# Inverse roots of all norms on ScalarE, shifts added by ScalarE, a seventh row buffer and a halved queue scratch

## The chip, the cores and the metric

The kernel runs on one core of a Trainium2 chip. The metric is device time in microseconds, the median of several runs; lower is better.

## The reference, cut to what matters

Two transformer blocks work on 512 positions of width 1024, all in float32. The change touches every norm and the gather of the experts:

```python
def rms_norm(x, g):
    y = xf * lax.rsqrt(jnp.mean(xf * xf, axis=-1, keepdims=True) + EPS)
    return y * g

# block one
h = rms_norm(x, norm1_g)
q, k = rms_norm(q, q_norm_g), rms_norm(k, k_norm_g)      # per head of 64
h2 = rms_norm(x, norm2_g)                                # ahead of w_up, w_down
# block two: the same norm with a gain and a shift that come from c
h  = rms_norm(x, g_norm1) * (1 + scale1) + shift1
q, k = rms_norm(q, g_q_sb), rms_norm(k, g_k_sb)
y_sb, y_ml = rms_norm(y_sb, g_out_sb), rms_norm(y_ml, g_out_ml) * sigmoid(o)
h2 = rms_norm(x, g_norm2) * (1 + scale2) + shift2
x  = x + gate2 * peer(h2, ...)
# peer: each position picks 128 of 16384 experts (8 heads, 16 each)
u, vv = expert_u[idx], expert_v[idx]                     # rows of 1024 numbers each
y = sum_k gate_k * gelu(h2 . u_k) * vv_k
```

## The kernel before

**The two halves.** The positions are worked in two halves of 256 (`half(0)`, `half(1)`). Within a half the activations lie transposed, as eight tiles of 128 features by 256 positions. Each half runs the same blocks of weights in the order of the list `SEQ`: query, key and value of block one (`Q1`, `K1`, `V1`), convolution inputs, attention with three weight products filled in between its heads, the projections, `UP` and `DN` (16 weight blocks each), then block two: `Q2`, `K2`, `QKM`, the two mixers with `V2`, `VM`, `OM` filled in, `WO2`, and the queries `PQ` of the expert choice. SyncE loads each weight block (1 MiB) into a ring of four as soon as the block four places back has been used. In half 0 there are 24 further blocks (`ADA`), which VectorE sums up for the modulation.

**A norm.** ScalarE squares the eight tiles, TensorE sums them over the partitions with a matrix of ones (bank 4), ScalarE takes `Sqrt` of the mean (`rms_root`, line 1096, or the end of `rms_squares`, line 1115), VectorE inverts it with `reciprocal` (`rms_inverse`, line 1638) and makes the eight tiles of `H`: `rms_scale` (line 1642) with one product each, `rms_modulate` (line 1648) with a product (line 1652) and, of the same engine, the addition of the shift (line 1655). TensorE's next weight block begins on tile 0 as soon as it is there and takes the tiles in order. There are eight such norms, numbered `a_` 0 to 7: 0 and 4 ahead of `Q1`, 1 and 5 ahead of `UP`, 2 and 6 ahead of `Q2`, 3 and 7 ahead of `PQ`. Those numbered 2, 3, 6 and 7 are modulated. In half 0 TensorE has other work beside norms 1 and 2: narrow products for the modulation (line 908).

**A head norm.** `head_squares` squares the tiles as they are evacuated, TensorE sums per head, `head_root` (line 1144) takes `Sqrt` of all heads at once, `head_inverse` (line 1658) inverts on VectorE, TensorE spreads the result over the partitions (`head_spreads`, line 642) and VectorE scales (line 1664). It is called for the queries during `K1`, for the keys during `V1`, and for block two during `QKM`. The two output norms of block two (lines 1401 and 1405 on ScalarE, 2011 and 2022 on VectorE) are small: 16 and 8 columns.

**The experts.** Each position needs 128 rows of u and v. For the four tiles of 128 positions these are 4 times 128 indirect DMAs of 1 MiB, called rows 0 to 511 below, issued by GpSimd (POOL) in that order; each brings one u and one v for 128 positions. VectorE takes the dot product with u (line 1537), ScalarE applies Gelu (line 1053), VectorE multiplies by the gate (line 1549), and adds v times that number (line 1566), or TensorE does so for every second row from row 198 on (line 563), for which ScalarE makes a diagonal matrix (line 1046). In half 1 the experts of the first half's positions run as steps of two rows, one after most weight blocks (`tick`; 99 steps). Their rows go round through six buffers of 8 KiB per partition (`uv0`). Rows 204 to 511 go round through 16 buffers: the six, the four weight blocks' places and six places of the activations. This table of buffers is written out ahead of time:

```python
NUV0, NUV1, WIDE = 6, 16, 204
CHANGE = ENTRIES.index(WIDE)
for _p, _e in enumerate(ENTRIES):
    _r = _p % NUV0 if _p < CHANGE else (_p - CHANGE + NUV0) % NUV1
```

GpSimd waits at `CHANGE` until TensorE has used the last weight block and the last scores are copied, and before each issue until the row that held the buffer has been consumed. It also stores the finished tiles of the output (line 517), 13 entries after their own; the buffer they are stored from is the one that the entry 16 places on takes.

## Time and profile before

| | us |
|---|---|
| median of three runs | 2686.62 (2684.66 to 2686.92) |
| the profiled execution, its device time | 2682.38 |
| its span, first to last instruction | 2680.7 |
| mean granted clock of TensorE | 0.901 |
| TensorE busy | 2168.2 (81%) |
| VectorE busy | 1762.0 (66%) |
| ScalarE busy | 640.1 (24%) |
| GpSimd busy | 785.5 (29%) |

Each engine's busy time is given against the span. The shares are averages over stages of different kind, so the stretches have to be read apart: the windows view gives busy times of each engine, TensorE's granted clock (1.00 is 2.4 GHz, 0.50 is 1.2 GHz) and the share of time in which the DMA engines moved data. In the timeline a number in brackets is the time that the engine stood idle before the instruction, with the instruction that ended it. One product of 128 by 128 by 256 in float32 shows as two MATMUL records of 0.215 us spacing at full clock.

### The profile page before, as it was taken

What the parts mean: (1) busy time and instruction counts of PE and PEld (TensorE: products, weight loads), DVE (VectorE), ACT (ScalarE), POOL (GpSimd) and SP (SyncE); (2) the same over time, 40 slices, a digit from 0 to 9 for tenths busy, and PEclk for the clock granted to TensorE, in tenths of its full rate; (3) what the DMA queues carried; (4) which work ended last, traced back from release to release, by engine and by line L of the source; (5) the groups of instructions that cost most, each with busy time, mean ns of one, the idle gap of its engine ahead of it and who ended that gap; (6) DMA issues with size and microseconds to landing.
All of it is one profiled execution on the core that took longest, in us unless ns stands there. A gap on an engine that the chain in (4) does not pass through costs nothing. (4 is left out here: it accounts for less than half of the span.)

```text
span 2680.7 us, 26294 instructions
## 1 busy us (share of the span) xinstructions
PE 2168.2 (81%) x9024; PEld 1627.7 (61%) x9024; DVE 1762.0 (66%) x3674; ACT 640.1 (24%) x1495; POOL 785.5 (29%) x541
## 2 busy tenths in 40 slices
PE   8999999999999999898999997988554554545544
PEld 6787788887788778677888776877111221212211
DVE  4662110002428769687777686676999999999987
ACT  2103302102332310563231134533111111111110
POOL 0000000000000234244433332224754555545552
PEclk9999999999999999899999998989877777778776
DMA  6774334443245699798999975468999999999997
GB/s 253 286 268 142 123 117 148 156 157 110 95 144 220 250 366 411 257 338 326 400 421 421 380 277 199 188 233 331 419 421 406 422 422 421 422 389 421 421 422 311
DMA packets 114868, 798.33 MB, mean 298 GB/s; under 512 B 13328, under 2 KB 16528, under 8 KB 19248
## 3 DMA queue, kind: packets, MB, share of 16 engines
q0 software_dynamic: 74736, 540.57, 49.6%
q1 hardware_dynamic: 40000, 256.09, 25.9%
q8 instruction: 72, 1.18, 0.2%
q14 instruction: 60, 0.49, 0.1%
HBM read 790.27 MB, written 6.34 MB: 297 GB/s over the span
## 5 line engine op out<-in xcount | busy, mean ns | idle before, releaser
L588 PE MATMUL PS<-reg,ring 128*128 128x256 f32 x6016 | 1360.9, 385 | 39.6 <-DVE reg L1655 10.8
L588 PEld LDWEIGHTS PS<-reg,ring 128*128 128x128 f32 x6016 | 1147.0, 193 | 222.5 <-issue 44.3
L536 POOL DMA_INDIRECT uv<-in_expert_uv,experts x318 | 520.9, 1638 | 1551.9 <-DVE experts L1519 842.7
L1566 DVE SCALAR_TENSOR_TENSOR acc<-uv,coef,acc 128x1024 f32<-128x1024 f32 x256 | 328.9, 1285 | 9.4 <-DVE coef L1549 0.3
L563 PE MATMUL PS<-reg,spare 128*128 128x512 f32 x224 | 156.6, 853 | 199.9 <-ACT spare L1046 199.9
L1537 DVE CUSTOM_DVE_ANT_0 uv<-uv,h_tok 128x1024 f32<-128x1024 f32 x222 | 263.7, 1220 | 36.5 <-DMA uv<-in_expert_uv,experts 36.2
L563 PEld LDWEIGHTS PS<-reg,spare 128*128 128x128 f32 x224 | 58.1, 275 | 297.4 <-issue 297.4
L563 PE MATMUL PS<-uv,spare 128*128 128x512 f32 x240 | 149.3, 768 | 95.8 <-ACT spare L1046 95.8
L1053 ACT ACTIVATE acts<-dots 128x2 f32<-128x2 f32 (+2 forms) x194 | 39.5, 204 | 762.0 <-DVE dots L1537 710.3
L536 POOL DMA_INDIRECT reg<-in_expert_uv,experts x114 | 159.3, 1398 | 206.2 <-PE PS L563 151.9
L563 PE MATMUL PS<-ring,spare 128*128 128x512 f32 x152 | 109.6, 874 | 85.0 <-ACT spare L1046 85.0
L563 PEld LDWEIGHTS PS<-uv,spare 128*128 128x128 f32 x240 | 54.7, 241 | 188.8 <-issue 188.8
L1841 DVE TENSOR_TENSOR reg<-PS,reg 128x256 f32<-128x256 f32 x16 | 6.5, 422 | 224.4 <-PE PS L588 224.4
L1537 DVE CUSTOM_DVE_ANT_0 reg<-reg 128x1024 f32<-128x1024 f32 x96 | 115.1, 1223 | 29.0 <-DMA reg<-in_expert_uv,experts 29.0
L563 PEld LDWEIGHTS PS<-ring,spare 128*128 128x128 f32 x152 | 40.0, 278 | 151.8 <-issue 151.8
L585 PE MATMUL PS<-ring,reg 128*128 128x256 f32 x512 | 121.1, 393 | 0.0
L536 POOL DMA_INDIRECT ring<-in_expert_uv,experts x80 | 96.6, 1207 | 75.0 <-PE PS L563 57.0
L1537 DVE CUSTOM_DVE_ANT_0 uv<-uv,reg 128x1024 f32<-128x1024 f32 x96 | 112.5, 1221 | 3.1 <-DMA uv<-in_expert_uv,experts 3.1
L585 PEld LDWEIGHTS PS<-ring,reg 128*128 128x128 f32 x512 | 98.9, 197 | 17.5 <-issue 3.9
L1053 ACT ACT_TABLE_LOAD x60 | 77.0, 1283 | 85.7 <-issue 57.2
L1735 DVE SCALAR_TENSOR_TENSOR uv<-ring,silu_c,uv 128x256 f32<-128x256 f32 x168 | 81.5, 485 | 6.0
L1549 DVE TENSOR_TENSOR coef<-acts,gates 128x2 f32<-128x2 f32 (+2 forms) x194 | 30.4, 157 | 82.5 <-ACT acts L1053 78.7
(264 smaller groups left out, 2133.1 us busy)
## 6 DMA issues: line engine op xcount, KB each, us to landing
ring<-in_weights SPq DMA_DIRECT2D x228, 1024.0 KB
uv<-in_expert_uv,experts POOLq DMA_INDIRECT x318
kv_half<-reg SPq DMA_DIRECT2D x1, 2052.0 KB, 11.2
reg<-kv_half SPq DMA_DIRECT2D x1, 2052.0 KB, 14.3
reg<-in_x_t SPq DMA_DIRECT2D x2, 1024.0 KB, 5.4
reg<-in_sub_t SPq DMA_DIRECT2D x2, 1024.0 KB, 4.9
toep<-rel_neg SPq DMA_DIRECT2D x16, 128.0 KB
x_tokens<-reg SPq DMA_DIRECT2D x2, 1024.0 KB, 10.0
```

The lines of the kernel that those rows point to most:

```text
L536: gp.indirect_dma_start(UV[r], None, a["expert_uv_2"], bass.IndirectOffsetOnAxis(ap=experts[:, e % 256:e % 256 + 1], axis=0))\
L563: mm = pe.matmul(PS[:, 6 + j, :], diag[:, n % 4, :], UV[BUF[s]][:, D + 512 * j:D + 512 * j + 512], start=begins, stop=ends, **LAX)
L585: mm = pe.matmul(out_tile(n, t), mv[:, t * P:(t + 1) * P], w, start=first and k == 0, stop=last and k == KT - 1)
L588: mm = pe.matmul(out_tile(n, t), w[:, t * P:(t + 1) * P], mv, start=first and k == 0, stop=last and k == KT - 1)
L1053: act.activation(acts[:, s0 % 16:s0 % 16 + s1 - s0], dots[:, s0 % 16:s0 % 16 + s1 - s0], ACT.Gelu)\
L1537: dve.tensor_tensor_reduce(out=u, in0=u, in1=H2[s // 256][:, s // NSLOT % 2, :], scale=1.0, scalar=0.0, op0=ALU.mult, op1=ALU.add, accum_o ...
L1549: dve.tensor_tensor(coef[:, q:q + w], acts[:, q:q + w], gates[:, s0 % 256:s0 % 256 + w], ALU.mult)\
L1566: dve.scalar_tensor_tensor(acc[:, :], v, c, acc[:, :], ALU.mult, ALU.add).then_inc(acc_done, 1)
L1735: dve.scalar_tensor_tensor(ac, ring[:, n % NRING, k, :], silu_c[:, k:k + 1], ac, ALU.mult, ALU.add)\
L1841: dve.tensor_tensor(x[:, k, :], out_tile(n, t), x[:, k, :], ALU.add).then_inc(evac_sem(n, t), 1)
```

## The change

The inverse root becomes two activations on ScalarE, `Ln` and then `Exp` with a factor of -0.5, for the eight norms, the six head norms and the two output norms in each half; VectorE's 18 reciprocals go. The shift of the modulated norms is added by ScalarE (`rms_shift`). All early loads of the `Sqrt` set become early loads of the set with `Exp` and `Ln`. In `head_spreads` TensorE now also waits for the scaling of the heads before at the first spread. The queue scratch, memory in which GpSimd's DMA queue keeps its descriptors, is declared at 8192 bytes per partition (16384 where nothing is declared), and the freed 8 KiB hold a seventh row buffer: 7 buffers up to row 203, 17 from row 204 on.

```diff
-NUV0, NUV1, WIDE = 6, 16, 204
+NUV0, NUV1, WIDE = 7, 17, 204
...
                 if j == 0:
                     pe.wait_ge(rr_done, 3 * hf + which + 1)
-                else:
+                if hf or which or j:
                     pe.wait_ge(hn_done, NQK * hf + 8 * which + 2 * j)
...
             def rms_root(a_):
                 act.wait_ge(rms_mm, KT * (a_ + 1))
-                act.wait_ge(h_done, KT * a_)
-                act.activation(rstd[:, :], PS[:, rms_bank(a_), 0:T], ACT.Sqrt, bias=epsc[:, :]).then_inc(rms_sqrt, 1)
+                if a_:
+                    act.wait_ge(h_done, KT * a_)
+                act.activation(rstd[:, :], PS[:, rms_bank(a_), 0:T], ACT.Ln, bias=epsc[:, :]).then_inc(rms_ln, 1)
+                act.wait_ge(rms_ln, a_ + 1)
+                act.activation(rstd[:, :], rstd[:, :], ACT.Exp, scale=-0.5).then_inc(rms_rec, 1)
+
+            def rms_shift(a_, g):
+                n0 = KT * (2 * (a_ // 4) + g)
+                for k in range(KT):
+                    act.wait_ge(h_pre, n0 + k + 1)
+                    act.activation(H[:, k, :], H[:, k, :], ACT.Identity, bias=mod[:, 24 * g + k:24 * g + k + 1]).then_inc(h_done, 1)
...
             def rms_squares(a_, src, ready):
-                ready_for(ACT.Sqrt)
+                ready_for_soft()
...
                 if at:
                     act.wait_ge(hb_done, at)
-                act.activation(hroot[:, :], PS[:, 5, 0:T], ACT.Sqrt, bias=epsc[:, :]).then_inc(rt_done, 1)
+                act.activation(hroot[:, :], PS[:, 5, 0:T], ACT.Ln, bias=epsc[:, :]).then_inc(rt_done, 1)
+                act.wait_ge(rt_done, 3 * hf + which + 1)
+                act.activation(hroot[:, :], hroot[:, :], ACT.Exp, scale=-0.5).then_inc(rr_done, 1)
...
                     rms_squares(2, X[0], lambda k: evac_wait(act, NO[0, DN, 4 * (k // 2) + 3], k % 2))
+                rms_shift(4 * hf + 2, 0)
...
-                act.activation(mean_sb[:, :], mean_sb[:, :], ACT.Sqrt, bias=epsc[:, :], scale=1.0 / HD2).then_inc(mix_root, 1)
+                act.activation(mean_sb[:, :], mean_sb[:, :], ACT.Ln, bias=epsc[:, :], scale=1.0 / HD2).then_inc(mix_root, 1)
+                act.wait_ge(mix_root, 2 * hf + 1)
+                act.activation(mean_sb[:, :], mean_sb[:, :], ACT.Exp, scale=-0.5).then_inc(mix_rec, 1)
...
                 if hf == 0:
-                    ready_for(ACT.Sqrt)
+                    ready_for_soft()
                     rms_root(4)
...
-            def rms_inverse(a_):
-                dve.wait_ge(rms_sqrt, a_ + 1)
-                dve.reciprocal(rstd[:, :], rstd[:, :]).then_inc(rms_rec, 1)
...
             def rms_modulate(a_, g, src):
-                n0 = KT * (2 * (a_ // 4) + g)
                 dve.wait_ge(rms_rec, a_ + 1)
                 for k in range(KT):
                     dve.scalar_tensor_tensor(H[:, k, :], src[:, k, :], gs[:, g, k:k + 1], rstd[:, :],
                                              ALU.mult, ALU.mult).then_inc(h_pre, 1)
-                    dve.wait_ge(h_pre, n0 + k + 1)
-                    dve.tensor_scalar(H[:, k, :], H[:, k, :], mod[:, 24 * g + k:24 * g + k + 1], None, ALU.add)\
-                        .then_inc(h_done, 1)
-
-            def head_inverse(hf, which):
-                dve.wait_ge(rt_done, 3 * hf + which + 1)
-                dve.reciprocal(hroot[:, :], hroot[:, :]).then_inc(rr_done, 1)
...
-    nc = bacc.Bacc("TRN2", target_bir_lowering=False, num_devices=1)
+    nc = bacc.Bacc("TRN2", target_bir_lowering=False, num_devices=1, dynamic_dma_scratch_size=8192)
```

## Rows read from the trace of the kernel before

**Rows 1.** The page: busy time of each engine, share of the span, instructions.
```profile
PE 2168.2 (81%) x9024; PEld 1627.7 (61%) x9024; DVE 1762.0 (66%) x3674; ACT 640.1 (24%) x1495; POOL 785.5 (29%) x541
```

**Rows 2.** Windows: stretch, length, five busy times, PE clock, DMA share, GB/s.
```profile
200.00:620.00 420.00, 416.12 (x2006) 355.79 (x2005) 45.77 (x168) 77.15 (x229) 0.00 (x0) 0.99 0.40 139
...
1300.00:1530.00 230.00, 226.64 (x1040) 198.44 (x1040) 167.78 (x269) 44.65 (x115) 90.80 (x58) 0.99 1.01 415
...
1870.00:2660.00 790.00, 409.33 (x615) 152.45 (x615) 726.54 (x1455) 126.46 (x321) 425.80 (x315) 0.76 1.01 417
```

**Rows 3.** Timeline at 1530: start, length, engine, line, operation, idle before it.
```profile
1530.17 0.47 ACT L1099 ACTIVATE rstd<-PS,singles 128x256 f32<-128x256 f32 x1 [0.79 <-PE PS L618]
1530.68 1.75 DVE L1640 RECIPROCAL rstd<-rstd 128x256 f32<-128x256 f32 x1 [1.75 <-ACT rstd L1099]
...
1532.99 0.35 DVE L1655 TENSOR_SCALAR reg<-reg,mod 128x256 f32<-128x256 f32 x1
...
1533.49 1.92 PE L588 MATMUL PS<-reg,ring 128*128 128x256 f32 x4 [3.35 <-DVE reg L1655]
...
1538.47 0.35 DVE L1655 TENSOR_SCALAR reg<-reg,mod 128x256 f32<-128x256 f32 x1
```

**Rows 4.** Timeline at 1302, the norm ahead of the up projection.
```profile
1302.18 1.19 PE L588 MATMUL PS<-reg,ring 128*128 128x256 f32 x2 [2.96 <-DVE reg L1645]
```

**Rows 5.** Timeline at 381 and 616: norms 1 and 2.
```profile
381.41 8.16 PE L908 MATMUL PS<-ones,uv 128*128 128x1 f32 x48
...
616.20 2.73 PE L908 MATMUL PS<-ones,uv 128*128 128x1 f32 x24
...
619.72 0.77 PE L588 MATMUL PS<-reg,ring 128*128 128x256 f32 x1 [0.78 <-DVE reg L1655]
```

**Rows 6.** Groups by line: an elementwise pass on ScalarE, buffer to buffer.
```profile
L1259 ACT ACTIVATE reg<-reg 128x256 f32<-128x256 f32 x64 | 26.8, 418 | 2.0
```

**Rows 7.** Windows around single PE gaps, columns as in Rows 2.
```profile
1534.00:1537.00 3.00, 3.00 (x8) 2.09 (x8) 2.86 (x9) 0.00 (x0) 0.00 (x0) 0.50 0.58 240
...
679.00:683.00 4.00, 3.35 (x17) 2.71 (x18) 3.44 (x9) 0.13 (x1) 0.00 (x0) 1.00 0.75 266
966.00:970.00 4.00, 3.82 (x13) 2.90 (x14) 3.10 (x6) 0.00 (x0) 0.51 (x1) 0.67 1.02 420
```

**Rows 8.** Timeline at 877, between the halves.
```profile
877.20 1.28 ACT L1085 ACT_TABLE_LOAD   x1
...
883.50 1.75 DVE L1640 RECIPROCAL rstd<-rstd 128x256 f32<-128x256 f32 x1
...
885.98 1.32 PE L588 MATMUL PS<-reg,ring 128*128 128x256 f32 x5 [0.29 <-DVE reg L1645]
```

**Rows 9.** Instructions of line 1053: table loads, ns min/median/max.
```profile
L1053 ACT ACT_TABLE_LOAD  x60: 1283/1283/1283, 897.3 to 2604.2; - x60
```

**Rows 10.** Timeline around the head spreads at 680, 966 and 1592.
```profile
679.65 0.70 PE L650 MATMUL PS<-hroot,spread 64*128 64x256 f32 x4 [1.25 <-DVE reg L1664]
...
964.38 1.75 DVE L1660 RECIPROCAL hroot<-hroot 128x256 f32<-128x256 f32 x1
...
966.18 0.70 PE L650 MATMUL PS<-hroot,spread 64*128 64x256 f32 x4 [1.73 <-DVE hroot L1660]
...
1591.88 1.14 PE L650 MATMUL PS<-hroot,spread 64*128 64x256 f32 x4 [3.99 <-DVE hroot L1660]
```

**Rows 11.** Windows of 10 us, columns as in Rows 2.
```profile
1850.00:1860.00 10.00, 10.00 (x54) 8.95 (x53) 9.58 (x24) 3.85 (x10) 3.23 (x3) 1.00 0.54 203
...
2380.00:2390.00 10.00, 7.16 (x11) 2.86 (x10) 9.79 (x21) 0.90 (x3) 3.00 (x3) 0.67 0.59 225
```

**Rows 12.** Timeline of POOL: the issue after the change of buffers, and a wait.
```profile
1877.13 0.94 POOL L536 DMA_INDIRECT ring<-in_expert_uv,experts  x1 [0.30 <-issue]
...
2386.39 0.94 POOL L536 DMA_INDIRECT reg<-in_expert_uv,experts  x1 [13.60 <-DMA out<-reg]
```

**Rows 13.** The page, by line: the gather issues of POOL.
```profile
L536 POOL DMA_INDIRECT uv<-in_expert_uv,experts x318 | 520.9, 1638 | 1551.9 <-DVE experts L1519 842.7
```

More of the change, by code:

```diff
@@ L334, in build @@
         x_loaded, par_loaded, w_if_loaded, consts = (sem(n) for n in ("x_loaded", "par_loaded", "w_if_loaded", "consts"))
-        rms_sq, rms_mm, rms_sqrt, rms_rec, h_pre, h_done = (sem(n) for n in (
-            "rms_sq", "rms_mm", "rms_sqrt", "rms_rec", "h_pre", "h_done"))
+        rms_sq, rms_mm, rms_ln, rms_rec, h_pre, h_done = (sem(n) for n in (
+            "rms_sq", "rms_mm", "rms_ln", "rms_rec", "h_pre", "h_done"))
         sq_done, ms_done, rt_done, rr_done, hb_done, hn_done = (sem(n) for n in (
@@ L1121, in rms_squares @@
                     act.activation(scr[:, k % 4, :], src[:, k, :], ACT.Square).then_inc(rms_sq, 1)
-                act.wait_ge(rms_mm, KT * (a_ + 1))
-                if a_:
-                    act.wait_ge(h_done, KT * a_)
-                act.activation(rstd[:, :], PS[:, 4, 0:T], ACT.Sqrt, bias=epsc[:, :]).then_inc(rms_sqrt, 1)
+                rms_root(a_)
             def head_squares(hf, kind, m0, raw, root=None):
@@ L1397, in half @@
                         ready_for_soft()
-                ready_for(ACT.Sqrt)
+                ready_for_soft()
                 pair_copy(3)
                 act.wait_ge(y2_sum, 4 * (hf + 1))
-                act.activation(mean_sb[:, :], mean_sb[:, :], ACT.Sqrt, bias=epsc[:, :], scale=1.0 / HD2).then_inc(mix_root, 1)
+                act.activation(mean_sb[:, :], mean_sb[:, :], ACT.Ln, bias=epsc[:, :], scale=1.0 / HD2).then_inc(mix_root, 1)
+                act.wait_ge(mix_root, 2 * hf + 1)
+                act.activation(mean_sb[:, :], mean_sb[:, :], ACT.Exp, scale=-0.5).then_inc(mix_rec, 1)
                 ml_abs_of(NML - 1)
@@ L1404, in half @@
                 act.wait_ge(ml_sq, 2 * NML * (hf + 1))
-                act.activation(mean_ml[:, :, :], mean_ml[:, :, :], ACT.Sqrt, bias=epsc[:, :], scale=1.0 / HDML).then_inc(mix_root, 1)
+                act.activation(mean_ml[:, :, :], mean_ml[:, :, :], ACT.Ln, bias=epsc[:, :], scale=1.0 / HDML).then_inc(mix_root, 1)
+                act.wait_ge(mix_root, 2 * hf + 2)
+                act.activation(mean_ml[:, :, :], mean_ml[:, :, :], ACT.Exp, scale=-0.5).then_inc(mix_rec, 1)
                 for m in range(4):
@@ L1413, in half @@
                     rms_squares(3, X[0], lambda k: evac_wait(act, NO[0, WO2, k // 2], k % 2))
+                rms_shift(4 * hf + 3, 1)
                 def score_copy(m):
@@ L1442, in half @@
                 if hf == 0:
-                    ready_for(ACT.Sqrt)
+                    ready_for_soft()
                     rms_root(4)
@@ L1761, in half @@
                     for i in range(4):
-                        if i == 1:
-                            head_inverse(hf, which)
                         for j in (2 * i, 2 * i + 1):
@@ L1832, in half @@
                     tick(hf, WO, i)
-                rms_inverse(4 * hf + 1)
                 rms_scale(4 * hf + 1, x, lambda k: col("norm2", k))
@@ L1850, in half @@
                     tick(hf, DN, i)
-                rms_inverse(4 * hf + 2)
                 rms_modulate(4 * hf + 2, 0, x)
@@ L1928, in half @@
                         silu(j - 1)
-                    if j == 2:
-                        head_inverse(hf, 2)
                     if j >= 4:
@@ L2009, in half @@
                 pair_sums(3)
-                dve.wait_ge(mix_root, 2 * hf + 1)
-                dve.reciprocal(mean_sb[:, :], mean_sb[:, :]).then_inc(mix_rec, 1)
                 ml_inverse(NML - 1)
@@ L2020, in half @@
                     dve.tensor_scalar(OMT[:, i, :], OMT[:, i, :], 0.5, 0.5, ALU.mult, ALU.add).then_inc(om_done, 1)
-                dve.wait_ge(mix_root, 2 * hf + 2)
-                dve.reciprocal(mean_ml[:, :, :], mean_ml[:, :, :]).then_inc(mix_rec, 1)
                 dve.wait_ge(mix_rec, 2 * hf + 2)
@@ L2040, in half @@
                     tick(hf, WO2, i)
-                rms_inverse(4 * hf + 3)
                 rms_modulate(4 * hf + 3, 1, x)
@@ L2055, in half @@
                     dve.wait_ge(top_done, 5 * 32)
-                    rms_inverse(4)
                     dve.wait_ge(tok_xpose, 4)
@@ L2063, in _ @@
             dve.wait_ge(consts, 18)
-            rms_inverse(0)
             rms_scale(0, X[0], lambda k: col("norm1", k))
```

## The prediction, made before the changed kernel was run

> **What bounds the kernel now.** I read the page first, then the windows by stage, then the timeline wherever TensorE stood still. TensorE is busy 81% of the span [rows 1], but that is an average over two regimes. Up to about 1870 us it is near its limit: 416 of 420 us in one long stretch of half 0, 227 of 230 us in half 1's up and down projections [rows 2]. After 1870 it is busy only half the time and the DMA engines are full, at 417 GB/s [rows 2]: the rest of the expert rows comes in, 1.049 MB each, so 2.51 us a row. The chain of waits reaches back only to about 1870 and runs over DMA, DVE and POOL. So the kernel is a product-bound part followed by a fixed amount of DMA, and what half 0 or half 1 loses between products is paid in full at the end, because the DMA-bound part starts that much later. The question is which of TensorE's stops the change shortens.
>
> **The eight norms.** At 1530 the whole sequence can be seen [rows 3]. The Sqrt begins at 1530.17, the reciprocal takes 1.75 us from 1530.68, the first product with its shift follows, and TensorE restarts at 1533.49, 3.32 us after the Sqrt's start and 3.35 us after its last work. The eight shifts begin 0.783 us apart (1532.99 to 1538.47, seven steps), as product and shift share VectorE; a tile's two records take TensorE 0.43 us at full clock. So it is fed by VectorE and gets the last tile at about 1538.9, 8.7 us after the Sqrt's start. In place of the reciprocal comes an Exp of the size of the Sqrt, 0.47 us [rows 3], with the same 0.04 us between dependent instructions: 1.28 us less until the first tile, in all norms. For the modulated ones the shift moves to ScalarE, where a pass of this size takes 0.42 us [rows 6] against 0.35 [rows 3]: 0.07 more once, but products and shifts now overlap, and tiles come every 0.43 us. First tile at 2.0 us after the Ln's start, last at 5.0: up to 3.7 us gained. Not all of it is usable. After the stop the granted clock is 0.50 (1.2 GHz) for some 3 us [rows 7], in which a tile takes TensorE 0.86 us. Now that hides behind VectorE's 0.78; with tiles every 0.43 us it is exposed, about four tiles by 0.43, 1.7 us. The stop shrinks from 3.35 to about 2.1 us, and a stop of 1.25 us left the clock at 1.00 while one of 1.73 us was followed by 0.67 over 4 us [rows 7, 10]. I take the drop to stay: 2.0 us each for norms 3, 6 and 7 (between 1.3 and 3.7).
>
> By number then. Norm 0, nothing beside it: 1.3. Norm 1: 0, since TensorE has 8.16 us of narrow products after the sum [rows 5]; they are the cover, and without them it would be 1.3. Norm 2: narrow products end at 618.93 and only 0.78 us of stop is left [rows 5]; with that and the quicker tiles 1.2 (0.8 to 3.1). Norm 3: 2.0. Norm 5: stop 2.96 us [rows 4], 1.3 (to 3.0 if the clock stays up). Norms 6 and 7: 2.0 each. Norm 4 lies between the halves [rows 8]: VectorE reaches the reciprocal only at 883.50, so all 1.75 us of it leave VectorE's path, but TensorE's own transposes hold it to 885.7; it stops 0.29 us. ScalarE's table load at 877.20, ahead of the copies on which these transposes wait, goes too (the set with Exp is in place), less the Exp's 0.5: 1.0 in all (0.3 to 1.5).
>
> **The head norms.** In half 0 those of `K1` and `V1` hold nobody up: 0. During `QKM` TensorE waits 1.25 us at 679.65 [rows 10] for a scaling that stands behind the reciprocal on VectorE: 1.25. In half 1 VectorE reaches the reciprocals late, behind expert steps, and TensorE waits 1.73 us at 966 and 3.99 us at 1592 [rows 10]. The first goes, as ScalarE has the root 7 us earlier: 1.7 (0, if the next wait, for the stored activations of half 0, takes it up; 3.4 with the clock drop [rows 7]). The second goes too, but VectorE is busy without a break there and TensorE ends the stage waiting for it, so only the reciprocal's 1.75 us less about 0.45 us of a later Tanh count: 1.3 (0.5 to 3).
>
> **What is added on ScalarE.** The set with Exp and Ln is in place in half 0; the load for attention is no longer made ahead but at the first Tanh, 1.28 us [rows 9], beside running products: cost 0.3 (0 to 1.3). In half 1 the roots come after a Gelu with no early load: one load as now, or two if Ln and Exp are served by two sets. The trace has no Ln in that place, so 0 to 1.28 us each; ScalarE is far from full and VectorE's reciprocal starts 9 us after the root at 955 [rows 10]: cost 0. The small output norms trade a 0.25 us reciprocal for an Exp that delays ScalarE's next work: 0.3 per half. TensorE's added wait for the scaling: VectorE's order held it before: 0.
>
> The load is 1.283 us here, and the next activation at 878.50 follows without pause [rows 8, 9]. The Trainium skill (ScalarE: Activation LUTs, What ACT_TABLE_LOAD costs) puts a switch at about 2.66 us, a drain included; by that the load removed before norm 4 would give 1.4 us more and the sum would be 19.3. The same page (Rules for kernel authors) gives additions to VectorE, not ScalarE. The rows agree that the pass is longer, 0.42 against 0.35; by that rule alone the 32 moved passes would cost 0.07 each, 2.2, instead of speeding up four norms, and the sum would be about 13. I go by the overlap.
>
> **The seventh buffer.** In half 1 each gather is issued one row earlier. TensorE does not wait for gathers there, and VectorE's waits for them lie in the projections, where products continue: 0. At the end of half 1 it counts. TensorE's last weight block ends at about 1863, but GpSimd issues row 204 only at 1877.13 [rows 12], since row 203 needs the buffer of row 197; with seven it needs that of 196, and one more row is in flight while DMA is at 0.54 [rows 11]. One row of 2.5 us is moved into idle time: 2.5 (0 to 2.5). In the DMA-bound part GpSimd stops twice for 13.60 us until a stored output tile has left its buffer [rows 12], once with DMA down to 0.59 over 10 us [rows 11]. One more buffer means one more row in the queue: 1.2 (0 to 4). The halved scratch: 0, see the third rival.
>
> **Sum.** Half 0: 1.3 + 0 + 1.2 + 1.25 + 2.0 + 1.0 - 0.3 - 0.3 = 6.15. Half 1: 1.7 + 1.3 + 2.0 + 1.3 + 2.0 - 0.3 = 8.0. End: 3.7. Together 17.9 us. The profiled execution took 2682.4 in device time (span 2680.7), so 2664.5; the median of the runs shown stands 4.2 us above it, so 2668.7. About 0.2% (5.4 us) is what a measurement of this kernel can tell from no change.
>
> **Rivals.** (1) The clock stays up: if stops of about 2 us no longer drop it, norms 3, 6 and 7 give 3.7, norm 5 3.0 and the stop at 966 3.4: 8.5 more, 2660. Against it speaks the 1.73 us stop. Chance 0.15. (2) Half 1's gains are swallowed: DMA is at 1.01 from 1300 to 1530 [rows 2] and VectorE runs at three quarters there; if expert steps, not products, pace half 1, only half 0 and the end remain, 9.9 us: 2677. For it: VectorE's late reciprocals. Against: TensorE's 227 of 230 us. Chance 0.16. (3) Slower: the smaller scratch makes GpSimd wait for room at each issue. An issue takes 1.64 us [rows 13] and 0.3 to the next; a row may take 2.51. From 0.57 us extra each it decides; at 1 us extra, 308 rows by 0.43 is 132 us, some 2800. For it speaks only that nothing in the trace shows how full the scratch gets. Chance 0.04. (4) The roots move but nothing is won: TensorE's stops are refilled by ScalarE, now holding sums, roots, shifts and Gelus; only norm 0, QKM and one of the others gain, 2682. Chance 0.05. The forecast itself has 0.60.
>
> The range, 2658 to 2678, takes in the first two and the bounds of the terms. Faster 0.92, same 0.05, slower 0.03.
>
> **What would show it.** TensorE's stop ahead of norms 3, 5, 6 and 7 at about 2.1, 1.7, 2.1, 2.1 us; products 0.40 us apart; the waits on `hroot` at line 650 gone in half 1; the gather of row 204 issued about 2.5 us earlier against the end of the last weight block; the span after that shorter by 1 to 4 us. Wrong would be: full clock right behind the norms (rival 1), unchanged time from 886 to 1870 (rival 2), or POOL issues above 2.2 us (rival 3).

## The result, and the profile after

| | us |
|---|---|
| before, median of six runs | 2685.85 (2682.17 to 2686.92) |
| after, median of six runs | 2651.93 (2647.15 to 2659.71) |
| ratio after to before | 0.9883, 95% interval 0.9864 to 0.9903 |
| forecast | 2668.7, range 2658 to 2678 |

The change gains 33.9 us by the medians (31.4 by the ratio, which pairs runs) where 17.9 were forecast; the measured median lies 6 us below the range. The profiled execution took 2648.0 us (span 2646.3), 34.4 us less than that of before, and stands 3.9 us below its median, as the other did (3.5).

First the page's busy times, beside [rows 1]: VectorE has lost 35.9 us of work, ScalarE has got 19.6, and TensorE, whose work is the same 9024 instructions, is busy 9.5 us less. That last difference goes with its clock, as the table below shows.

```profile
PE 2158.7 (82%) x9024; PEld 1622.4 (61%) x9024; DVE 1726.1 (65%) x3624; ACT 659.7 (25%) x1537; POOL 796.3 (30%) x541
```

Next the windows from the start to TensorE's first late product (the first of line 563 in the DMA-bound part, at 1878.4 before and 1847.7 after). The columns are those of [rows 2]; TensorE's idle time is the length less its busy time. Before:

```profile
0.00:1878.40 1878.40, 1756.72 (x8409) 1474.90 (x8409) 1025.88 (x2214) 514.35 (x1176) 364.50 (x230) 0.97 0.66 251
```

After:

```profile
0.00:1847.70 1847.70, 1745.01 (x8408) 1469.18 (x8408) 990.22 (x2164) 534.01 (x1218) 365.85 (x230) 0.97 0.67 255
...
1275.50:1502.70 227.20, 224.97 (x1040) 197.44 (x1040) 166.47 (x268) 45.15 (x117) 90.20 (x58) 1.00 1.01 419
```

Of the 30.7 us gained up to there, TensorE's idle time gives 19.0 (121.7 to 102.7) and its busy time 11.7. The remaining 3.7 us come after it. The table sets this against the forecast, stage by stage. A stage runs from the start of one norm's root to the start of the next (the first from the kernel's start). The last two columns tell where it came from: by how much TensorE's idle time fell, and by how much the time at a granted clock of 0.50. An engine that works through such time works at half speed, so half of the last column is time gained, 10.2 us in all.

| stage | before | after | gained | forecast | idle, less | at 0.50, less |
|---|---|---|---|---|---|---|
| start to norm 1 | 381.6 | 375.2 | 6.4 | 1.0 | 5.5 | 3.4 |
| norm 1 to 2 | 234.8 | 231.5 | 3.3 | 0 | 0 | 6.8 |
| norm 2 to 3 | 189.4 | 183.8 | 5.6 | 2.15 | 2.3 | 6.8 |
| norm 3 to 4 | 72.8 | 70.8 | 2.0 | 2.0 | 1.3 | 0 |
| norm 4 to 5 | 420.6 | 414.3 | 6.3 | 2.7 | 3.1 | 6.8 |
| norm 5 to 6 | 230.9 | 227.1 | 3.8 | 1.3 | 2.0 | 3.4 |
| norm 6 to 7 | 265.5 | 263.9 | 1.6 | 3.0 | 3.5 | -7.2 |
| norm 7 to first late product | 82.7 | 81.2 | 1.5 | 2.0 | 1.2 | 0.4 |
| from there to the end | 802.3 | 798.6 | 3.7 | 3.7 | | |

Norm 6 in the timeline after, to be set beside [rows 3]: the first product starts 2.13 us after the Ln, TensorE stands still for 2.17 us instead of 3.35, and the shifts follow each other on ScalarE, eight in 3.30 us.

```profile
1502.66 0.47 ACT L1101 ACTIVATE rstd<-PS,singles 128x256 f32<-128x256 f32 x1 [0.79 <-PE PS L618]
1503.17 0.42 ACT L1103 ACTIVATE rstd<-rstd 128x256 f32<-128x256 f32 x1
1503.62 3.26 DVE L1662 SCALAR_TENSOR_TENSOR reg<-reg,gs,rstd 128x256 f32<-128x256 f32 x8 [2.19 <-ACT rstd L1103]
1504.14 3.30 ACT L1109 ACTIVATE reg<-reg,mod 128x256 f32<-128x256 f32 x8 [0.55 <-DVE reg L1662]
...
1504.79 8.44 PE L588 MATMUL PS<-reg,ring 128*128 128x256 f32 x38 [2.17 <-ACT reg L1109]
```

The other stops of TensorE that changed, in the timeline after: norm 5 (2.96 us in [rows 4]), the head spreads of half 1 (3.99 in [rows 10]) and the first product of attention in half 1.

```profile
1057.57 1.19 PE L678 MATMUL PS<-reg 64*128 64x256 f32 x2 [5.80 <-DVE reg L1812]
...
1277.12 1.10 PE L588 MATMUL PS<-reg,ring 128*128 128x256 f32 x4 [1.62 <-DVE reg L1656]
...
1566.50 1.22 PE L650 MATMUL PS<-hroot,spread 64*128 64x256 f32 x4 [5.42 <-DVE reg L1667]
```

GpSimd's issues, to be set beside [rows 12]: the first into the ring, 3.5 us ahead of the first late product (1.25 before), and the two behind the stores of output tiles.

```profile
1844.21 1.98 POOL L536 DMA_INDIRECT ring<-in_expert_uv,experts  x1 [0.30 <-issue]
...
2026.42 0.94 POOL L536 DMA_INDIRECT reg<-in_expert_uv,experts  x1 [13.68 <-DMA out<-reg]
...
2352.91 0.94 POOL L536 DMA_INDIRECT uv<-in_expert_uv,experts  x1 [14.56 <-DMA out<-uv]
```

Last the head root of half 1 after a Gelu. It takes two table loads, each followed within 0.02 us by its activation. The Trainium skill (ScalarE: Activation LUTs, What ACT_TABLE_LOAD costs) adds a drain of about 1.4 us to a load; the trace shows none here. TensorE waits for none of it.

```profile
903.04 1.28 ACT L1156 ACT_TABLE_LOAD   x1
904.34 0.47 ACT L1156 ACTIVATE hroot<-PS,singles 128x256 f32<-128x256 f32 x1
904.83 1.28 ACT L1158 ACT_TABLE_LOAD   x1
906.12 0.42 ACT L1158 ACTIVATE hroot<-hroot 128x256 f32<-128x256 f32 x1
```

### The profile page after: what moved, and what is told of

It is laid out like the page before. It is cut to its first block and busy times, and to the rows that moved or that the text cites. A ratio compares the mean times of both kernels' runs of the same rounds, so it can differ in the third digit from the quotient of the medians.

```text
span 2646.3 us, 26290 instructions
## 1 busy us (share of the span) xinstructions
PE 2158.7 (82%) x9024; PEld 1622.4 (61%) x9024; DVE 1726.1 (65%) x3624; ACT 659.7 (25%) x1537; POOL 796.3 (30%) x541
## 5 line engine op out<-in xcount | busy, mean ns | idle before, releaser
L588 PEld LDWEIGHTS PS<-reg,ring 128*128 128x128 f32 x6016 | 1142.5, 192 | 204.9 <-issue 35.9
L536 POOL DMA_INDIRECT uv<-in_expert_uv,experts x329 | 529.6, 1610 | 1610.6 <-DVE experts L1534 862.1
L563 PE MATMUL PS<-uv,spare 128*128 128x512 f32 x260 | 177.2, 832 | 169.9 <-ACT spare L1046 169.9
L563 PE MATMUL PS<-reg,spare 128*128 128x512 f32 x212 | 140.8, 814 | 118.6 <-ACT spare L1046 118.6
L563 PEld LDWEIGHTS PS<-uv,spare 128*128 128x128 f32 x260 | 64.9, 265 | 278.1 <-issue 278.1
L536 POOL DMA_INDIRECT reg<-in_expert_uv,experts x107 | 150.3, 1405 | 110.1 <-PE PS L563 39.9
L563 PE MATMUL PS<-ring,spare 128*128 128x512 f32 x144 | 99.6, 842 | 87.0 <-ACT spare L1046 87.0
L1552 DVE CUSTOM_DVE_ANT_0 uv<-uv,reg 128x1024 f32<-128x1024 f32 x104 | 123.0, 1220 | 15.5 <-DMA uv<-in_expert_uv,experts 15.5
L536 POOL DMA_INDIRECT ring<-in_expert_uv,experts x76 | 107.6, 1416 | 73.6 <-PE PS L563 47.2
L1552 DVE CUSTOM_DVE_ANT_0 reg<-reg 128x1024 f32<-128x1024 f32 x89 | 105.2, 1220 | 10.6 <-DMA reg<-in_expert_uv,experts 10.6
```

Source lines behind the costliest of these rows:

```text
L536: gp.indirect_dma_start(UV[r], None, a["expert_uv_2"], bass.IndirectOffsetOnAxis(ap=experts[:, e % 256:e % 256 + 1], axis=0))\
L563: mm = pe.matmul(PS[:, 6 + j, :], diag[:, n % 4, :], UV[BUF[s]][:, D + 512 * j:D + 512 * j + 512], start=begins, stop=ends, **LAX)
L588: mm = pe.matmul(out_tile(n, t), w[:, t * P:(t + 1) * P], mv, start=first and k == 0, stop=last and k == KT - 1)
L1552: dve.tensor_tensor_reduce(out=u, in0=u, in1=H2[s // 256][:, s // NSLOT % 2, :], scale=1.0, scalar=0.0, op0=ALU.mult, op1=ALU.add, accum_o ...
```

## The experiments

### The change in its parts

Four kernels: the changed one with six rows; the kernel before with the rows alone; before with the scratch alone; and the changed one with VectorE's shift.

```diff
# e1b: changed kernel
-NUV0, NUV1, WIDE = 7, 17, 204
+NUV0, NUV1, WIDE = 6, 16, 204
-    nc = bacc.Bacc(..., dynamic_dma_scratch_size=8192)
+    nc = bacc.Bacc(...)
# e2b: kernel before
-NUV0, NUV1, WIDE = 6, 16, 204
+NUV0, NUV1, WIDE = 7, 17, 204
# e2b and e3b: kernel before
+    nc = bacc.Bacc(..., dynamic_dma_scratch_size=8192)
# e4b: changed kernel, in rms_modulate; both calls of rms_shift go
+                    dve.wait_ge(h_pre, n0 + k + 1)
+                    dve.tensor_scalar(H[:, k, :], H[:, k, :], mod[:, 24 * g + k:24 * g + k + 1], None, ALU.add)\
+                        .then_inc(h_done, 1)
```

Roots and shift with six rows:

> The changed kernel with six row buffers (16 late) and the scratch left undeclared: roots on ScalarE and shifts by ScalarE alone. Theory (the gain lies in TensorE's stops before 1870 us and in the clock that follows them): the stretch up to the last norm's Ln is as in the changed kernel (1766 us), the time 2655, with 3 to 4 us given back after it. Rival (the excess over the forecast comes from the seventh buffer): 2668, the forecast's sum without its end term being 2672.

The rows alone:

> The kernel before with seven row buffers (17 late) and the scratch at 8192, roots and shifts untouched. Theory: only the end gains, 3.7 us as forecast, so 2682. Rival (the buffer carries the excess): 2670 or less, with half 1 shorter between 886 and 1796 us.

The scratch alone:

> The kernel before with the scratch at 8192 and nothing else. Theory: nothing changes, 2686 within 3 us, GpSimd's issues 1.64 us each. Rival (a small scratch makes GpSimd wait at issues and the seventh buffer pays for it): 2690 or more, longer issues. If it is faster by 3 us or more, the scratch itself is part of the gain.

The shift on VectorE:

> The changed kernel with the shift added by VectorE again, roots still on ScalarE. Theory (overlap of product and shift is worth 0.4 us per tile while TensorE runs at full clock, half of that at 0.50): norms 2, 3, 6 and 7 each lose 1.5 to 3 us, 8 us together, so 2660. Rival (only the stop counts, the tiles' spacing is hidden): within 1 us of the changed kernel. Rival of the Trainium skill's rule that additions belong to VectorE: faster than the changed kernel.

Measured: roots and shift alone 2661.85 us, ratio 0.9921 (0.9897 to 0.9945), so about 21 us. The rows alone 2677.99, 0.9979 (0.9966 to 0.9992), 5.6 us. The scratch alone 2683.31, 1.0005 (0.9992 to 1.0018): nothing, with issues of 1634 ns against 1638 [rows 13]. The shift on VectorE 2652.42, 0.9895 (0.9874 to 0.9916): not to be told from the changed kernel.

(In microseconds of gain the ratios are used from here on, since they pair runs on one chip; the kernel before alone ranged from 2670.8 to 2691.9 us over its runs.) **Roots.** 21 us is half as much again as the 14.2 forecast for them, and lies between the two expectations (2655 and 2668). The profile has the last norm's Ln at 1779.4 us, not at 1766. It also says that this excess is not the clock. Up to the first late product TensorE's idle time is 16.8 us less than before (104.9), its busy time only 1.0 (1755.75), and the clock stood at 0.50 for longer than before, 136 us against 129:

```profile
0.00:1860.60 1860.60, 1755.75 (x8408) 1477.59 (x8409) 990.68 (x2164) 534.15 (x1218) 362.99 (x229) 0.96 0.67 253
```

**Rows.** More than the 3.7 forecast, though the interval takes that in. The sum of the two parts is 27, the whole 31; the intervals are wider than that difference, so the times don't show that anything is left over. **The scratch** costs nothing, so the rival by which GpSimd waits for room is out. **The shift** was worth nothing that can be measured as the change stands, against the expectation of 8 us and for its rival.

The kernel with the scratch alone has the instructions of the kernel before, and yet its profiled execution is 7.0 us shorter. Two stages hold 6.4 of it. From 100 to 160 us TensorE is busy 51.36 us before and 54.25 here, as weights come late (stops of 1.10, 3.46 and 4.08 us before). And the stage from norm 1 to norm 2, all busy in both, takes 234.8 and 231.5 us. Windows before:

```profile
100.00:160.00 60.00, 51.36 (x220) 42.62 (x220) 40.80 (x91) 5.72 (x13) 0.00 (x0) 0.94 0.81 302
...
381.60:616.40 234.80, 234.80 (x1090) 207.29 (x1090) 8.77 (x19) 29.57 (x75) 0.00 (x0) 0.98 0.40 142
```

Windows with the scratch alone:

```profile
100.00:160.00 60.00, 54.25 (x241) 45.23 (x240) 44.37 (x99) 5.70 (x13) 0.00 (x0) 0.97 0.86 320
...
378.50:610.00 231.50, 231.50 (x1090) 204.17 (x1089) 8.68 (x19) 29.48 (x75) 0.00 (x0) 0.99 0.41 144
```

So 3.1 us of the first stage's gain and the 3.3 of the second can come about with no change at all. From norm 1's narrow products on the clock stood at 0.50 for 10.2 us before, and for 3.4 with the scratch alone and after; of the profiles of all kernels with the new roots some show 234.8, some 233.2, some 231.5 for that stage.

### The seventh buffer early or late, and the head roots

```diff
# e5: changed kernel
-NUV0, NUV1, WIDE = 7, 17, 204
+NUV0, NUV1, WIDE = 6, 17, 204
-        uv0 = sb("uv0", [P, NUV0, 2 * D])
+        uv0 = sb("uv0", [P, NUV0 + 1, 2 * D])
-        UV = [uv0[:, r, :] for r in range(NUV0)] + ...
+        UV = [uv0[:, r, :] for r in range(NUV0 + 1)] + ...
# e6: changed kernel; head_inverse on VectorE at its places of before
-                act.activation(hroot[:, :], PS[:, 5, 0:T], ACT.Ln, bias=epsc[:, :]).then_inc(rt_done, 1)
-                act.wait_ge(rt_done, 3 * hf + which + 1)
-                act.activation(hroot[:, :], hroot[:, :], ACT.Exp, scale=-0.5).then_inc(rr_done, 1)
+                act.activation(hroot[:, :], PS[:, 5, 0:T], ACT.Sqrt, bias=epsc[:, :]).then_inc(rt_done, 1)
```

> The changed kernel with six row buffers up to row 203 and 17 from row 204 on: the seventh buffer in the DMA-bound part alone. Theory (in half 1 the seventh buffer takes away VectorE's waits for gathers in front of attention, so the stop at the first attention product is 5.8 us with it and 7.1 without): that stop is back at 7.1 us, half 1 is 1.3 us longer plus up to 3 us of low clock, the end as in the changed kernel; 2655. Rival (only the end gains from the buffer): 2652, the stop unchanged.

> The changed kernel with the head norms' roots as before (Sqrt on ScalarE, reciprocal on VectorE), the eight norms and the shifts as changed. Theory: the stops of 1.25 us in QKM of half 0 and of 1.7 us at the head spreads of half 1 with its low clock come back, 1.3 + 3.4 less 0.5 that the later wait had taken up, so 4 us and 2656. Rival (head roots were hidden behind expert steps): within 1 us of the changed kernel.

**Late only**: 2661.47 us, 0.9927 (0.9902 to 0.9952), no better than six rows throughout (0.9921) and 6 us above its theory. The stop at attention is back (first row below). From the first late product to the end it takes 800.8 us, what the kernel with six rows takes too (800.7), where the changed one takes 798.6. So what the buffer brings comes from its work up to row 203, at the end too: that is the prefetch that I had priced at 2.5 us. The part priced at 1.2, fewer stops behind an output store, is not there: the changed kernel still waits 13.68 and 14.56 us for the stores.

Timeline of the late-only kernel at attention, and before norm 6, where a late gather holds VectorE 2.63 us, VectorE holds the residual, and TensorE waits 1.64 us for the squares:

```profile
1065.81 1.19 PE L678 MATMUL PS<-reg 64*128 64x256 f32 x2 [7.07 <-DVE reg L1812]
...
1497.27 1.23 DVE L1552 CUSTOM_DVE_ANT_0 uv<-uv,h_tok 128x1024 f32<-128x1024 f32 x1 [2.63 <-DMA uv<-in_expert_uv,experts]
...
1499.34 0.70 PE L618 MATMUL PS<-scr,ones_d 128*128 128x256 f32 x2 [1.64 <-ACT scr L1094]
```

VectorE's waits for gathers ahead of attention in half 1 are what the stop there goes with. The line shows them before, 886 to 1083 us (total, number, longest). After, from 868 to 1062, there is none, nor in the kernel with the rows alone, whose stop is 5.81 us instead of 7.07:

```profile
DVE uv L1537 <- DMA uv<-in_expert_uv,experts: 3.1, 2, 2.2
```

How the wait becomes the stop is not shown. The wait is 3.1 us in all before, 1.7 with six rows and the new roots, 0.9 in the late-only kernel, and the stop is 7.07 us each time. It is 7.07 in the kernel with the head roots back as well, which has seven rows and one such wait of 0.67 us. In the kernels with bridges ahead of the norms there is no such wait, and the stop is 6.4. So the buffer doesn't take the wait away by itself, and more than the wait sets the stop.

The stage from norm 5 to norm 6 shows the parts working together. With six rows the new roots bring it from 230.9 to 230.1 and 230.3 us, with seven old roots to 229.9, with both to 227.1, in the changed kernel and in four others with both; three more show 227.8, 228.8 and 228.9. DMA moves 419 GB/s there after (second row of the windows after) and 415 before, as much as in the DMA-bound part, 417 [rows 2]. The two kernels with six rows fit the reading that DMA holds the stage: late only, TensorE works 1.4 us less there than with six rows throughout (225.57 against 226.93, as the clock stayed up) and stands still 1.6 us more (4.7 against 3.2). With seven rows and the new roots it stands still 2.2.

**Head roots back**: 2658.61 us, 0.9902 (0.9880 to 0.9924), 5 us more than the changed kernel by the ratios, 4 expected. The intervals overlap, so it stays open. 3.8 us of the profile's difference lie from norm 4 to norm 5, where the stop at attention is back at 7.07 us too, which the theory did not count. Its trace has the stops of 1.25 us in QKM and 1.73 at the head spreads again.

### Holding the clock

After the changed kernel's stops the clock still falls in many places, and I took that for what a stop really costs. The next kernels put products of ones by ones, into a half bank that nobody reads, where TensorE would stand still. Nothing is taken out of the computation.

```diff
# e7: changed kernel
+            def bridge(n):
+                for _ in range(n):
+                    pe.matmul(PS[:, 5, T:2 * T], ones_d[:, :], ones_1[:, :], start=True, stop=True)
...
                     residual_blocks(WO, 5, lambda k: GCM[:, k, :])
+                    bridge(3)
...
                     rms_sum(6, 7)
+                    bridge(4)
...
                     rms(3)
+                    bridge(4)
...
                     residual_blocks(WO2, 7, lambda k: mixed(hf, k), ready=mixed_ready)
+                    bridge(4)
# e8: besides
+                if hf and which == 2 and j == 1:      # in head_spreads
+                    bridge(10)
...
+                bridge(7)                             # ahead of mixers(hf)
```

> The changed kernel with idle products of TensorE (ones by ones into an unused half bank) in the stops ahead of norms 3, 5, 6 and 7: four each (1.7 us at full clock), three at norm 5. Nothing is taken out of the computation. Theory (what follows a stop is a fall of the granted clock, and it is the stop that causes it): the clock stays at 1.00 behind norms 3 and 7, where the changed kernel shows 0.50 for 3.4 and 6.8 us, 1.7 and 3.4 us gained in those two, so 2647 to 2649. Rival (the clock falls by itself at such places): the same low stretches, the products cost up to 0.4 us each where they outlast the stop, 2652 to 2654.

> The same and also seven such products ahead of the mixers in both halves (stops of 3.4 us) and ten ahead of the second head spread of half 1 (stop of 5.4 us). Theory: three more low stretches (3.4, 6.8 and 6.8 us) go, 6 us more than with the bridges at the norms, so 2641 to 2644. Rival: no gain beyond noise.

Measured 2648.62 us, 0.9872 (0.9848 to 0.9896), and 2639.11, 0.9839 (0.9816 to 0.9862): 3 and 12 us below the changed kernel by the ratios. The first lies in its theory's range, but its interval and that of the changed kernel overlap. The second is clear, and 1.9 us below what the theory asked for. In the windows it has 3.95 us more busy time than the changed kernel (it also has its added products) and 13.9 us less idle time:

```profile
0.00:1837.80 1837.80, 1748.96 (x8487) 1475.25 (x8487) 990.09 (x2164) 534.21 (x1218) 366.28 (x231) 0.98 0.68 257
```

Norm 3's stage takes 69.1 us, 3.7 less than before: the very figure that the prediction gave for a norm with the clock held up. At norm 7 the bridge worked in part. It comes behind a stop of 2.60 us at the sums and runs at the low clock itself (8 records in 3.41 us against 1.89 at norm 6), so that it outlasts the stop that it fills: the first product comes 3.0 us after the Ln instead of 2.1. But the clock is back 3.4 us after the Ln instead of 6.5, and the stage takes 80.1 us against 81.2 (79.9 with the bridges at the norms alone). Timeline of this kernel:

```profile
1501.45 1.89 PE L611 MATMUL PS<-ones,ones_d 128*128 128x256 f32 x8
1503.78 2.40 PE L588 MATMUL PS<-reg,ring 128*128 128x256 f32 x10 [0.44 <-ACT reg L1120]
...
1756.52 1.13 PE L622 MATMUL PS<-scr,ones_d 128*128 128x256 f32 x4 [2.60 <-ACT scr L1105]
1757.49 3.41 PE L611 MATMUL PS<-ones,ones_d 128*128 128x256 f32 x8
1760.70 4.47 PE L588 MATMUL PS<-reg,ring 128*128 128x256 f32 x19
```

### What the clock hides: the shift again, and the kernel before with bridges

The bridges of e8 with the shift of e4b; and bridges in the kernel before:

```diff
# e10: the kernel of e8, with e4b's lines in rms_modulate and no rms_shift
# e11: kernel before; bridge(n) as above, in the same four places
+                    bridge(6)       # norm 5
+                    bridge(7)       # norms 3, 6 and 7
...
+                if hf and which == 2 and j in (1, 2):
+                    bridge(2 if j == 1 else 5)
...
+                bridge(6)           # ahead of mixers(hf)
```

> The kernel with all bridges up to the mixers (2639), but with the shift added by VectorE. Theory (overlap of product and shift was worth little because TensorE ran at 0.50 behind the stop and took 0.86 us per tile; with the clock held at 1.00 it takes 0.43 while VectorE needs 0.78): norms 3, 6 and 7 lose 2.4 us each, 5 to 7 us in all, so 2644 to 2646. Rival (the overlap is worth nothing in any case): 2639 within 2 us.

> The kernel before with bridges at the same norms (seven, six, seven and seven products ahead of norms 3, 5, 6 and 7), two and five ahead of the second and third head spread of half 1 and six ahead of the mixers in both halves. Theory (a large part of what the change gained was clock that its shorter stops no longer lost): the kernel before gains 8 to 12 us by bridges alone, so 2674 to 2678, and the change is worth 35 us on top. Rival (the clock is lost anyway, or the bridges only shift it): 2683 or more.

With the shift on VectorE 2647.11 us, 0.9873 (0.9851 to 0.9894), 8 us above its like by the medians and 9 by the ratios, more than the 5 to 7 expected, where without bridges the two could not be told apart. The windows show why. In the 6 us from norm 6's first product both have the clock at 1.00; with the shift on VectorE TensorE gets through 17 records, with ScalarE's through 28. Shift on VectorE:

```profile
1507.90:1513.90 6.00, 5.41 (x17) 2.58 (x18) 5.57 (x18) 0.00 (x0) 0.00 (x0) 1.00 0.93 388
```

Shift on ScalarE:

```profile
1503.70:1509.70 6.00, 5.92 (x28) 5.25 (x29) 5.78 (x12) 3.39 (x9) 1.78 (x1) 1.00 0.88 365
```

The stage from norm 3 to norm 4 takes 71.3 against 69.1 us: 2.2, where 2.4 were expected. The stages behind norms 6 and 7 take 3.8 and 1.2 us more, that behind norm 2 0.7 less. Another 3.7 of the 8.8 us between the two profiles lie from norm 4 to norm 5, where no shift is added (416.7 against 413.0); there the clock stood at 0.50 for 6.8 us more. So the shift itself accounts for about 7 us in the profiles. The Trainium skill (ScalarE: Activation LUTs, Rules for kernel authors) gives additions to VectorE. The runs say: without bridges it makes no difference that can be measured, with the clock held the rule costs some 7 us here, because it is the chain through one engine that counts and not the pass.

The kernel before with bridges: 2672.78 us, 0.9964 (0.9949 to 0.9980), 9.6 us by the ratio and 7.1 by the medians, where 8 to 12 were expected. So the clock behind stops is worth about that much there too.

This pair also tells how much of the change's gain is such clock. With bridges in both kernels the change is worth 33.7 us by the medians (2672.78 to 2639.11) and 34 by the ratios, as much as the 31 without bridges. If the excess over the forecast were only clock lost at these stops, the bridges would have taken it away. Some of what replaces it is known: with the clock held the quicker tiles are worth more (norm 3's stage goes from 72.8 to 69.1 us, 3.7 instead of 2.0).

### How far it goes

```diff
# e9: the kernel of e8; bridge(n, bank)
+                        bridge(5)                     # ahead of norm 7's sum 6
+                    bridge(12)                        # in attention, half 1, ahead of scores(0)
+                    bridge(7, N_ITEMS % 3)            # ahead of transposes(N_ITEMS - 1), half 1
+                        bridge(24, 4)                 # ahead of sums(2) of the mixers, half 1
+                        pe.wait_ge(ml_y, 2 * (mb + e))
+                        bridge(8 if e == 3 else 3)    # ahead of ml_values(1 to 3), half 1
+                bridge(2 if hf else 7, 7)             # ahead of the mixers' last transposes
# e12: the kernel of e9
-                    bridge(12)
-                    bridge(7, N_ITEMS % 3)
+                    bridge(11)                        # ahead of attention(hf), half 1, before its waits
+                        bridge(5, N_ITEMS % 3)        # one item earlier
```

> The kernel with all bridges so far, and more of them in half 1: twelve ahead of the attention products, seven ahead of the last probabilities' transposes, 24 in the stop of 11.4 us inside the mixers, three, three and eight ahead of the later gate-weighted values, five ahead of the last sums of norm 7, and seven (half 0) or two (half 1) ahead of the mixers' last transposes. Theory (low clock behind stops is what is left to win): low stretches of 6.8, 13.7, 10.2 and three of 3.4 us shrink, 8 to 15 us less than with the bridges before (2639), so 2624 to 2631. Rival (half 1 is by now paced by expert steps on VectorE and by gathers, not by TensorE): 2636 to 2640, with stops longer where the clock is higher.

> The kernel with wide bridges, two of them moved: the products ahead of attention in half 1 (now eleven) stand before TensorE's waits for the convolved values instead of behind them, where they ran after the stop of 5.8 us and cost 6.9 us of their own; and the seven ahead of the last transposes, 3.2 us in a stop of 1.0, become five ahead of the stop of 3.3 us that is one item earlier. Theory (the wide bridges lost there what they won in the mixers): the stage between the norms ahead of Q1 and UP in half 1 takes 411 to 413 us instead of 421, and the time is 2628 to 2633. Rival (half 1 is paced by expert steps, so that clock won in one place returns as a stop in the next): 2637 to 2640.

The wide kernel took 2639.52 us, 0.9843 (0.9819 to 0.9868), no better than e8. Its rival said that half 1 was paced by something else. In part it was a slip of mine: twelve products stood behind TensorE's waits and not ahead of them. They ran after the stop, 6.86 us long, and seven others took 3.19 us in front of a stop that is 1.0 in the changed kernel:

```profile
1061.09 6.86 PE L611 MATMUL PS<-ones,ones_d 128*128 128x256 f32 x24 [5.81 <-DVE reg L1837]
```

Moved, they lie in the stop and leave 1.62 us of it, and the stage from norm 4 to 5 is down from 421.2 to 414.0 us:

```profile
1050.63 4.91 PE L611 MATMUL PS<-ones,ones_d 128*128 128x256 f32 x22
1057.16 0.67 PE L686 MATMUL PS<-reg 64*128 64x256 f32 x2 [1.62 <-DVE reg L1837]
```

That kernel takes 2636.95 us, 0.9823 (0.9805 to 0.9841), 16 us below the changed one by the ratios (15 by the medians), and is the fastest here. It stayed above the 2628 to 2633 of the theory, next to the 2637 to 2640 of the rival, and is only 2.6 us below the wide kernel by the medians (the profiled execution of that one was its slowest) and 2.2 below e8. So putting the slip right did not bring the 8 to 15 us that the wide bridges were built for. The stage from norm 6 to 7 is the one that won, 251.2 us against 256.0 in e8 and 263.9 in the changed kernel; that from norm 4 to 5 is 1.0 us longer than in e8 (413.0), so in attention the bridges took what they gave. The rival has that stage and the time for it; no run shows that a stop grew because of the clock, and what holds half 1 here stays open.

## Why the prediction was wrong

**Right.** What bounds the kernel, and that TensorE's stops before the DMA-bound part are paid in full: 30.7 us gained up to the first late product, none of it lost behind it. The single norms by their stops: 1.62, 2.16, 2.17 and 2.16 us at norms 5, 3, 6 and 7, against 1.7 and three times 2.1 forecast. Norm 3's term, 2.0, was measured at 2.0. The 1.25 us in QKM of half 0 and the 1.73 at the first head spreads of half 1 went; of the latter the next wait, for the stored activations, took back 0.4 (2.78 us for 2.40). The row prefetched ahead of the change of buffers: GpSimd's first issue into the ring came 2.3 us earlier against the first late product, 2.5 forecast. The scratch at 0.

**The step that failed first**: "I take the drop to stay: 2.0 us each for norms 3, 6 and 7", and with it that the clock was counted at these norms and as an upper bound at norm 5 and at the stop at 966, but at no other stop. The sum was one of stops; a stop also costs what the clock loses behind it, and the drop did not stay everywhere. Up to the first late product the clock was at 0.50 for 129 us before and 109 after, which is 10.2 of the 16.5 us by which the profiles exceed the forecast. The low stretches can be paired one by one:

- Behind stops that the new roots shortened or took away, three stretches of 3.4 us went: at norms 5 and 6, and at the spreads at 966. That is 5.1 us gained. Rival 1, which had 0.15, had these as its terms and is what half happened: the clock fell at norms 3 and 7 all the same.
- Behind three stops that the roots do not touch, 3.4 us each went: at the mixers' first stop and their last transposes in half 0, and at attention in half 1. That is 5.1 us more, which the sum had nowhere.
- From the head spreads of half 1 to norm 7 there are 10.2 us more of it, 3.4 at the spreads and 6.8 in the mixers. That is 5.1 us lost.
- Another 10.2 us less lie in the first two stages, 5.1 us gained; 6.8 of these 10.2 are also gone in the kernel with the scratch alone, with no instruction changed.

So the clock step is wrong, but it does not carry the whole miss. With six rows the profile lost more clock than the kernel before and the roots gave 21 us even so, and with bridges in both kernels the change was worth 34. Of those 21 the profile's stages give 4.5 for the first, where 1.0 was forecast and late weights play a part, and 4.8 from norm 2 to 3, where 2.15 was; the stages from there to the first late product are near their terms or below. How much of the miss is clock on average is not known.

In the stage from norm 2 to 3 (3.4 us over the forecast) the clock is higher behind the mixers' first stop and behind that at their last transposes, whose own stops are as long as before (3.44 us, and 3.27 before against 3.37). Windows there before:

```profile
689.00:703.00 14.00, 10.63 (x37) 8.56 (x38) 4.67 (x12) 6.71 (x11) 0.00 (x0) 0.76 0.22 75
769.00:783.00 14.00, 13.40 (x56) 11.23 (x55) 5.74 (x18) 3.30 (x13) 0.00 (x0) 0.76 0.66 244
```

and after:

```profile
676.30:690.30 14.00, 10.57 (x41) 8.63 (x42) 4.74 (x12) 6.76 (x11) 0.00 (x0) 0.88 0.20 75
755.30:769.30 14.00, 13.63 (x63) 11.68 (x64) 5.76 (x17) 4.94 (x15) 0.00 (x0) 0.88 0.76 278
```

But no price per stop would have been right either. Norm 5's stop is 1.62 us in all kernels with the new roots and no bridge; behind it the clock is at 1.00 in the changed kernel and low in the one with six rows. The windows of 3 us from its first product, after:

```profile
1277.00:1280.00 3.00, 2.88 (x13) 2.57 (x14) 2.96 (x9) 0.00 (x0) 0.00 (x0) 1.00 1.02 429
```

and with six rows:

```profile
1287.00:1290.00 3.00, 3.00 (x8) 2.42 (x9) 2.96 (x9) 0.00 (x0) 0.00 (x0) 0.58 0.99 418
```

I had set the limit between 1.25 and 1.73 us from two rows. The Trainium skill (TensorE: Matmul & The Clock Gate, Part 1: The HAM clock gate) says of a kernel's start that the same kernel shows a different number of slow products from run to run. No run here measures that at the start; the pair of kernels above, identical but for the scratch, shows the like between norms 1 and 2, with 3.3 us.

**The second**: "TensorE does not wait for gathers there, and VectorE's waits for them lie in the projections, where products continue: 0". VectorE waited 3.1 us for two gathers ahead of attention too, and without them TensorE's stop there is 1.27 us shorter (7.07 to 5.80 us at line 678). In the projections its waits do reach TensorE, through residual and squares (1.64 us in the late-only kernel). From norm 5 to 6 idle time fell by 2.0 us, of which the shorter stop at the norm is 1.34; the rest, 0.65, is these waits, as with the rows alone. The larger part of the excess there, 3.8 us against 1.3, is the clock behind norm 5 (1.8 us less busy time). The rows alone gave 5.6 us where 3.7 stood, though the 1.2 for the stores was wrong: the stops for a store are as long as ever, and the last stage owes the rest of its 3.7 us to the new roots (802.1 and 802.3 us with the old roots and six rows, 800.7 and 800.8 with the new).

**The third, with the other sign**: 1.3 us for QKM in half 1. The stage from norm 6 to 7 gave 1.6 us where 3.0 were forecast. The stop moved. TensorE no longer waits for the root at the first spread, but 5.42 us for the scaling at the second and 3.44 at the mixers: 8.9 us instead of 10.0, since VectorE is late there anyway; and the clock was low for 6.8 us twice instead of 3.4 and 6.8.

**Neither right nor wrong**: the first two stages gave 9.7 us, 8.7 over the forecast. Up to 6.4 us of that the scratch-only kernel shows with no instruction changed, late weights and clock. What the new roots do there on average one profile per kernel can't tell. The medians still differ by 34 us, so not all of the 34 in the profiles is chance; how much of it is clock in half 0 stays open.

**The range** took the clock's gain (8.5 us) as its lower end and did not add the other upper bounds to it. With those of norms 2 and 4, of QKM and of the stores (6.9 us in all) it would have reached about 2653, still 1 us above the median measured.

## What to carry to other kernels

Price a stop of TensorE as its length and the low clock behind it: look at the granted clock in the microseconds after each stop before and after, and keep it as a term with a range of its own, since a stop of the same length lost it in one kernel's profile and not in another's. Where a stop can't be removed, idle products inside it (ahead of the engine's wait, never behind it) gave 12 to 16 us here. And a faster link that changes nothing, like the shift on ScalarE, may only be hidden by another: it was worth about 7 us once the clock was held. Before a cause is named from one profile, set beside it the profile of a program with the same instructions: here two of them differed by 7.0 us, late weights and clock.

## What was not expected of the hardware

A program with the same instructions and another scratch size showed 231.5 us where the kernel before showed 234.8, for a stretch in which TensorE never stops. In both, 48 products one column wide stand at its start. Before, the clock fell 2.3 us into them and stood at 0.50 for 10.2 us, and they took 8.16 us; with the scratch alone it fell at their end, for 3.4 us, and they took 5.42. A bridge that starts behind a stop of 2.6 us ran at the low clock itself, outlasted the stop that it filled and still gave 1.1 to 1.3 us, as the clock rose 3 us sooner.
